# Writing out the loop over pairs of mixer heads on four engines of a two-layer trunk kernel

## What is computed

```python
for l in range(DEPTH):                       # DEPTH = 2
    x = x + 0.5 * swiglu(rmsnorm(x, ...), ...)          # feed-forward 1, D_FF = 2816
    x = x + hybrid_mixer(rmsnorm(x, mix_norm[l]), ...)  # the part that matters here
    x = x + 0.5 * swiglu(rmsnorm(x, ...), ...)          # feed-forward 2
return rmsnorm(x, final_norm)
```

## Time and profile before

| what | us |
|---|---|
| three executions | 3022.87, 3027.3, 3028.06 |
| median | 3027.3 |
| span of the profiled execution | 3025.0 |
| TensorE matmuls busy in it | 2886.5 (95%) |
| VectorE, ScalarE, GpSimd busy | 1623.9, 1111.0, 333.2 |

### The profile page before, as it was taken

One profiled execution on the slowest core, in us unless ns is written; L12 is line 12 of the kernel. 1 busy time (PEld: TensorE's weight loads), 2 busy tenths in 40 slices (PEclk: granted clock), 3 DMA queues, 4 the chain that ended last, 5 costly groups with the idle time before them and its releaser, 6 DMA issues.

```text
span 3025.0 us, 41101 instructions
## 1 busy us (share of the span) xinstructions
PE 2886.5 (95%) x14080; PEld 2393.0 (79%) x14080; DVE 1623.9 (54%) x2435; ACT 1111.0 (37%) x1647; POOL 333.2 (11%) x292
## 2 busy tenths in 40 slices
PE   7999979999999999999999999699899999999999
PEld 6888857888887888888778887478788878888887
DVE  5554226878787344553255532368788863545532
ACT  4232234545554233322132221355455532332321
POOL 1000021211123010000000000112112220100000
PEclk9999989999999999999999999799999999999999
DMA  4333245544653433333233333656666734333332
GB/s 144 97 97 91 71 99 126 105 109 109 101 115 81 103 92 90 96 97 96 75 105 97 95 91 63 111 107 110 98 112 96 127 76 105 90 91 97 95 96 66
DMA packets 479208, 296.72 MB, mean 98 GB/s; under 512 B 12180, under 2 KB 462868, under 8 KB 479092
## 3 DMA queue, kind: packets, MB, share of 16 engines
q1 hardware_dynamic: 462964, 236.63, 32.0%
q0 software_dynamic: 16128, 58.73, 10.1%
HBM read 234.51 MB, written 2.10 MB: 78 GB/s over the span
## 4 chain that ended last, share of the span: by engine, by line
PE 85%; DMA 4%; issue 4%; DVE 3%; ACT 3%; POOL 0%; DVEq 0%; ACTq 0%; SPq 0%; POOLq 0%
PE bank L414 83%; DMA raw<-in_w_in 3%; PE bank L542 2%; DMA w_lo<-raw 1%; ACT w_hi L751 1%; DVE cacc L1176 1%; ACT w_lo L753 1%; ACT NT L886 0%; DVE NT L1295 0%; DVE w_lo L1004 0%; DVE XT L1300 0%; DMA raw<-in_ffn_w_gate 0%; ACT dec L889 0%; ACT qd L890 0%; PE bank L478 0%
## 5 line engine op out<-in xcount | busy, mean ns | idle before, releaser
L414 PE MATMUL bank<-h_hi,w_hi 128*128 128x512 f32 x2432 | 968.3, 398 | 26.3 <-DVE h_lo L1031 13.5
L414 PE MATMUL bank<-h_lo,w_hi 128*128 128x512 f32 x2432 | 970.6, 399 | 0.0
L414 PE MATMUL bank<-h_hi,w_lo 128*128 128x512 f32 x2432 | 967.9, 398 | 0.0
L751 ACT ACTIVATE w_hi<-raw 128x1024 fp32r<-128x1024 f32 x448 | 472.0, 1057 | 703.9 <-PE bank L414 635.2
L1004 DVE TENSOR_TENSOR w_lo<-raw,w_hi 128x1024 fp32r<-128x1024 f32 x336 | 412.5, 1229 | 553.8 <-ACT w_hi L751 552.8
L414 PEld LDWEIGHTS bank<-h_hi,w_hi 128*128 128x128 f32 x2432 | 461.1, 190 | 117.0 <-DVE h_lo L1031 15.0
L414 PEld LDWEIGHTS bank<-h_lo,w_hi 128*128 128x128 f32 x2432 | 462.3, 190 | 86.3
L414 PEld LDWEIGHTS bank<-h_hi,w_lo 128*128 128x128 f32 x2432 | 461.5, 190 | 85.6
L1176 DVE SCALAR_TENSOR_TENSOR cacc<-c_raw,ncol,cacc 128x512 f32<-128x512 f32 x464 | 380.6, 820 | 9.5
L414 PE MATMUL bank<-act_hi,w_hi 128*128 128x512 f32 x704 | 279.1, 396 | 0.0
L414 PE MATMUL bank<-act_lo,w_hi 128*128 128x512 f32 x704 | 279.1, 396 | 0.0
(11 more groups left out here) (236 smaller groups left out, 3181.3 us busy)
## 6 DMA issues: line engine op xcount, KB each, us to landing
raw<-in_w_in SPq DMA_DIRECT2D x128, 512.0 KB, 8.4
w_lo<-raw POOLq DMA_DIRECT2D x112, 512.0 KB, 6.7
raw<-in_ffn_w_gate SPq DMA_DIRECT2D x88, 512.0 KB, 3.8
raw<-in_ffn_w_up SPq DMA_DIRECT2D x88, 512.0 KB, 3.8
raw<-in_ffn_w_down SPq DMA_DIRECT2D x64, 512.0 KB, 3.7
raw<-in_ffn_w_down SPq DMA_DIRECT2D x32, 384.0 KB, 3.2
raw<-in_w_a_out SPq DMA_DIRECT2D x16, 512.0 KB, 3.8
raw<-in_w_b_out SPq DMA_DIRECT2D x16, 512.0 KB, 3.7
```

The lines of the kernel that those rows point to most:

```text
L414: return nc.tensor.matmul(o, a, b, start=start, stop=stop, **kw)
L751: nc.scalar.activation(w_hi[c % SLOTS][:, :], raw[c % SLOTS][:, :], ACT.Copy).then_inc(hi_done, 1)
```

## The change

On TensorE, VectorE, ScalarE and GpSimd the loop of three passes becomes a Python loop, so that its body is in the program three times, with numbers in place of the loop's register. Nothing is computed in another order, and no wait is added or taken away. The sync engine keeps its loop, and so do all feed-forward stages, the output stage and the two layers.

```diff
@@ TensorE
                 head((G0, 6, l * 8 + 1), l * 8, before=False)
-                with pe.Fori(0, 3) as p:
+                for p in range(3):
                     for half in range(2):
                         head((G0 + p * 3 + 3, 6 * half, l * 8 + p * 2 + (2 + half)), l * 8 + p * 2 + (1 + half))
                 head((G0 + 12, 0, None), l * 8 + 7)
@@ ScalarE
-                with act.Fori(0, 3) as p:
+                for p in range(3):
@@ VectorE
-                with dve.Fori(0, 3) as p:
+                for p in range(3):
@@ GpSimd
-                with pool.Fori(0, 3) as p:
+                for p in range(3):
```

## The result

The changed kernel takes 2971.6 us (median of 5 executions, 2969.3 to 2973.5) against 3027.3 us (5 executions, 3022.9 to 3032.4); the ratio is 0.9822, with an interval of 0.9811 to 0.9834. The forecast was 2999.8 us and the range 2992 to 3010: the sign was right, and the gain of 55.7 us is twice the 27.5 us that were summed.

What follows compares the result with a forecast made beforehand. TensorE, busy 2886.5 of 3025.0 us, was taken as the bound. Four jumps back gave 27.5 us and the other terms nothing, so 3027.3 - 27.5 = 2999.8 us, range 2992 to 3010.

Steps and rivals of the forecast that it cites:

- The four jumps back: VectorE's loop over head pairs, before `hs`, two jumps per layer: not jumping back was to win 27.5 us of TensorE's time.
- The name of the pause: VectorE's issue wait before `hs`: said to be fetching the code of its pass anew after each taken branch.
- Added code at nothing: Passes two and three in both layers: TensorE's 24 more q8 code packets, fetched behind its own matmuls, were to cost nothing.
- (a): VectorE's straight code is fetched too late in places, once per layer: 13.8 us come back, 3013.6 us; chance 0.08.
- (b): TensorE waits for code at each of 24 added q8 packets in passes two and three: 45.1 us, 3044.9; chance 0.03.
- The loop's own instructions at nothing: Branches and register steps of the head loop on VectorE and TensorE: 2.8 us if all on the path, taken as nothing.
- Rival (c): The wait before `hs` comes from the place in the program, not the jump, and stays: 3027 us; chance 0.03.
- outside the heads everything as before: A sign of being right: all stages other than the mixer's heads keep their times, with no gain or loss.
- the third term: Code added by writing out the passes, mainly TensorE's 24 more q8 packets: fetching hidden behind matmuls, cost put at nothing.
- The range: Whole kernel: 2992 to 3010 us, from gains of 24.2 to 30.3 us, widened 5 us below and 7 us above.

## Why the prediction was right, and where it was wrong

- **The four jumps back, 27.5 us: right.** The heads gave 27.6 us, the place and the engine are those of the chain, and VectorE's loop alone gives it all. Taking TensorE's lost time and not VectorE's idle 24.2 us was right for this trace. That the two sizes agree to 0.1 us says little, since the same trace of before stands in both. Over both layers the heads take 821.8 to 831.1 us in the ten traces with VectorE's loop and 801.3 in the changed kernel, so in other executions the pauses are worth 20 to 30 us.
- **The name of the pause: right.** A code fetch was argued from q14's packets. The runs show that the pause belongs to VectorE's jump, and the traces that one 8 KB code packet stands in each of 40 pauses, 1.8 to 2.1 us ahead of its end. The Trainium skill (Runtime: NRT & Kernel Launch, Instruction fetch mechanics) calls such a wait an instruction-fetch stall, and the traces agree.
- **Added code at nothing: right for its fetching.** 24 more q8 packets stand in the changed kernel, its heads keep 56.8 us (one in each layer 57.1), and rivals (a) and (b) did not happen. The later head periods that were long, in other programs, have a late weight in the chain. For the time as a whole the term was not nothing, as the step that failed says.
- **The loop's own instructions at nothing: right here,** with no more than 0.1 us in the two stretches of heads beyond the 27.5. The later 0.36 us a head from writing out the layers shows that VectorE's register arithmetic isn't free where it stands ahead of a step that TensorE waits for.
- **Rival (c): wrong,** as given.
- **The step that failed** is one that the prediction took for granted: "outside the heads everything as before". With it failed the third term, the code that is added to TensorE's program, which was put at nothing because only its fetching was thought of. TensorE's loop alone written out makes the kernel 1.0% faster (ratio 0.9899, some 30 us) with the pauses still in it. The sum had no term for a stage whose instructions stay the same. The stage from the first `w_in` load to `hs` of head 0 gained 7.6 and 22.9 us, 30.6 in all. It had 198.2 us in the kernel before, and I never read it, because no instruction in it changed. Its 42 GB/s stood in the trace of before, a pace that the same DMA does not have elsewhere: four units of the gate matrix, read alone, land in 9.2 us and four of `w_in` in 28.9. That this pace changes with TensorE's program could not be read from that trace.
- **The range** took its lower end from the spread of the executions (5.2 us). That spread is of one program. It tells nothing of what another program does to a stage that it leaves alone, which was 30 us here.

What stays open is why the reads differ. Shown: it is reads of `w_in` and not the four units of the gate matrix that were tried; it needs no other traffic; it goes with TensorE's program, not in step with its length; the order within a unit hardly matters. That the program moves arrays in device memory, or maps them differently, is one reading that fits. It is not shown: no run has an address, and the two tries at moving arrays (their order, one array more) changed nothing. The Trainium skill (DMA: Bandwidth & Descriptors, Latency and other measured facts) tells of copies whose partitions' rows lie a large power of two apart: 103 GB/s at a pitch of 4 MiB against 207 at 512 KiB, with aliasing of memory channels named as an inference. That row does not explain `w_in`. Its partitions' rows are 8208 x 4 = 32,832 bytes apart, and the eight rows of one partition 128 times that, which is 4 MiB and 8 KiB, while the page's 4 MiB pitch with 4 KiB more ran at full speed (214 GB/s). A pitch is also the same in all programs here, and the pace is not.

## What to carry to other kernels

Ask of a loop's jump back which engine fetches its pass again: here it was VectorE with 363 instructions in a pass, each of its jumps cost TensorE 1.9 to 11.6 us in the profiled execution, and that one engine's loop written out was enough. When a change makes a program longer or shorter, look whether loads that it never touches have changed speed. Read the stages that wait for memory in the trace before, and when a result doesn't match the sum, cut both traces at landmarks before looking for a story: half of this gain was in a stage that no line of the change reaches. A gain of that second kind can be lost again by the next edit, as it was when TensorE's layers were written out.

## What was not expected of the hardware

The same four loads of 512 KB, 512 bytes a packet, took from 15.3 to 35.0 us in eleven programs. The kernel before and the changed one repeated their own times in a second build and with all engines idle (28.9 and 34.5 us against 29.2 and 35.0; 19.8 and 19.5 against 19.6 and 18.8). In 40 jumps back VectorE went on 1.8 to 2.1 us after the start of one 8 KB code packet, and what made a pause 2.7 or 10.6 us long was how late that packet started. Three pieces of register arithmetic on VectorE, 40 ns each in the records, delayed a step by 0.17 us (0.21 against 0.04), and TensorE waited for it in every head.
